# The even layer's mixer in another order: index products inside the projection of queries and keys, index sums on VectorE alone, conv ahead of values, three attention heads inside the value projection, and a masked minimum as softmax bias

## What is computed

```python
proj = h @ w_in      # q, k, v (512 each), q_idx 1024, k_idx 64, w_idx 16, gate_b, gate_c, x_in (512 each)
q, k, q_idx, k_idx = partial_rope(...)
rel   = relu(einsum('bqhd,bsd->bqhs', q_idx, k_idx))        # 16 index heads, 64 wide
score = where(causal, einsum('bqhs,bqh->bqs', rel, w_idx), -inf)
sel   = top_k(score, 64)                                    # keys that each query may see
attn  = softmax(where(selected & causal, q @ k.T * 64**-0.5, -inf)) @ v     # 8 heads
conv  = gate_b * causal_conv_width_3(gate_c * x_in)
mix   = concatenate([attn, conv]) @ w_out
x     = x + rms_norm(mix) * gain
```

## Time and profile before

| | |
|---|---|
| median of 3 runs | 1078.1 us (1076.7 to 1078.5) |
| the profiled execution | 1079.2 us, its span 1077.4 us |
| TensorE busy, matmuls | 1041.1 us, 97% |
| VectorE busy | 660.3 us, 61% |
| ScalarE busy | 562.0 us, 52% |
| GpSimd busy | 103.3 us, 10% |
| DMA | 176.3 MB, 164 GB/s on average |
| granted TensorE clock, mean of the span | 0.989 |

### The profile page before, as it was taken

The page is one execution under the profiler, slowest core; times in us unless marked ns, Lnnn a source line. Parts: engine busy times, 40 slices in busy tenths (PEclk is TensorE's granted clock), DMA queues, the critical chain, the costliest instruction groups (busy, mean ns, idle before and its releaser), DMA issues.

```text
span 1077.4 us, 13860 instructions
## 1 busy us (share of the span) xinstructions
PE 1041.1 (97%) x5074; PEld 872.3 (81%) x5074; DVE 660.3 (61%) x1034; ACT 562.0 (52%) x853; POOL 103.3 (10%) x128
## 2 busy tenths in 40 slices
PE   7999999999999999999989999999998999999997
PEld 6888878887888888788867888888898878888886
DVE  5575665456645555758686855555469767555453
ACT  6466455436554544644544755444366557444541
POOL 2010101001000000202740100000051001000000
PEclk9999999999999999999979999999999999999999
DMA  8746126414545455544422465454246035555521
GB/s 335 283 161 232 53 99 228 148 40 176 183 182 219 157 195 195 194 154 155 157 78 78 183 228 185 171 200 173 91 145 233 29 118 215 179 200 186 195 79 39
DMA packets 28462, 176.29 MB, mean 164 GB/s; under 512 B 3249, under 2 KB 3393, under 8 KB 9985
## 3 DMA queue, kind: packets, MB, share of 16 engines
q1 hardware_dynamic: 26784, 170.08, 43.4%
q0 software_dynamic: 1456, 5.48, 1.4%
q10 hardware_dynamic: 176, 0.13, 0.0%
HBM read 174.62 MB, written 1.05 MB: 163 GB/s over the span
## 4 chain that ended last, share of the span: by engine, by line
PE 83%; DVE 9%; issue 3%; ACT 3%; POOL 2%; DMA 1%; SPq 0%; DVEq 0%; ACTq 0%; POOLq 0%
PE PS L1560 71%; PE PS L1664 3%; PE PS L1629 3%; PE PS L1681 2%; DVE w_lo L1041 2%; PE PS L1771 2%; ACT w_hi L598 2%; DVE w_lo L1035 1%; PE PS L1672 1%; DMA x<-in_x 1%; DVE arena L1074 1%; POOL h L505 1%; DVE h L1406 1%; POOL arena L498 1%; ACT work L678 0%
## 5 line engine op out<-in xcount | busy, mean ns | idle before, releaser
L1041 DVE SCALAR_TENSOR_TENSOR w_lo<-w_raw,gcol,w_hi 128x512 fp32r<-128x512 f32 (+4 forms) x318 | 264.8, 890 | 206.5 <-ACT w_hi L598 205.9
L598 ACT ACTIVATE w_hi<-w_raw,gcol 128x512 fp32r<-128x512 f32 (+4 forms) x326 | 244.5, 817 | 103.1 <-PE PS L1560 102.2
L1560 PE MATMUL PS<-w_hi,hT_hi 128*128 128x512 f32 (+2 forms) x888 | 243.4, 394 | 6.9 <-DVE hT_lo L1056 2.6
L1560 PE MATMUL PS<-w_hi,hT_lo 128*128 128x512 f32 (+2 forms) x888 | 236.3, 386 | 0.0
L1560 PE MATMUL PS<-w_lo,hT_hi 128*128 128x512 f32 (+2 forms) x888 | 234.9, 385 | 0.3 <-DVE w_lo L1041 0.2
L1560 PEld LDWEIGHTS PS<-w_hi,hT_hi 128*128 128x128 f32 x888 | 162.1, 190 | 38.5 <-DVE hT_lo L1056 3.5
L1560 PEld LDWEIGHTS PS<-w_lo,hT_hi 128*128 128x128 f32 x888 | 165.0, 189 | 33.8 <-DVE w_lo L1041 0.9
L1560 PEld LDWEIGHTS PS<-w_hi,hT_lo 128*128 128x128 f32 x888 | 165.8, 190 | 32.8
L1035 DVE TENSOR_TENSOR w_lo<-w_raw,w_hi 128x2048 fp32r<-128x2048 f32 (+1 forms) x70 | 135.7, 1954 | 83.6 <-ACT w_hi L598 83.6
L598 ACT ACTIVATE w_hi<-w_raw 128x2048 fp32r<-128x2048 f32 (+1 forms) x70 | 114.6, 1643 | 106.7 <-PE PS L1560 106.7
L1560 PE MATMUL PS<-w_hi,gT_hi 128*128 128x512 f32 x408 | 113.9, 392 | 0.0
(11 more groups left out here) (169 smaller groups left out, 821.9 us busy)
## 6 DMA issues: line engine op xcount, KB each, us to landing
w_raw<-in_w SPq DMA_DIRECT2D x64, 1024.0 KB, 4.8
w_raw<-in_w_gu SPq DMA_DIRECT2D x22, 1024.0 KB, 4.8
w_raw<-in_w_in SPq DMA_DIRECT2D x11, 1024.0 KB, 7.4
w_raw<-in_w_dn SPq DMA_DIRECT2D x22, 512.0 KB, 5.1
w_raw<-in_w_mem_k SPq DMA_DIRECT2D x4, 1024.0 KB, 4.8
w_raw<-in_w_out SPq DMA_DIRECT2D x4, 1024.0 KB, 4.8
w_raw<-in_w_cq SPq DMA_DIRECT2D x4, 1024.0 KB, 4.8
w_raw<-in_w_mem_v SPq DMA_DIRECT2D x4, 1024.0 KB, 4.9
```

The source lines that it names most:

```text
L598: ins = act.activation(high, source, ACT.Copy, scale=1.0 if col is None else gcol[:, col + TURNED * k:col + TURNED * k + 1])
L1041: ins = dve.scalar_tensor_tensor(out=lo, in0=raw, scalar=gcol[:, col + TURNED * k:col + TURNED * k + 1], in1=hi, op0=ALU.mult, op1=ALU.sub ...
L1560: mm = pe.matmul(bank(t, j)[:, 0:width], rows[:, kc0 + k, tok], w[:, s, at:at + width], start=begin and i == 0, stop=end and i == 2)
```

## The change

It does the same matmuls, transposes and reads, in another order and with some of the elementwise work on another engine:

- **Index.** `turn_index` moves to (0, 1) of the projection of queries and keys, and the 12 banks of index products stand in it three at a time. ScalarE copies all turned banks there. Its relus write to 12 places (`INDEX_HOME`), and wait for no sum. VectorE makes the sums of both tiles; GpSimd's `index_sum` is gone. Tile 0's search stands between the sums of banks 5 and 6, tile 1's behind the rotation of queries and keys.
- **Conv ahead of values.** `w_cx` is loaded and projected ahead of `w_vg`, both unit by unit (`by_unit`: both tiles of a unit one after the other). The turn of queries and keys stands in the conv projection, that of gate_c * x_in in the value projection.
- **Heads inside.** Scores of heads 0, 1 and 2 and the turn of head 0 stand inside the value projection.
- **Gate.** It is turned behind head 3 into the free PSUM banks 0 and 1, and ScalarE copies it. The conv's multiply waits for it (`gate_copied`), and the subtraction to `hT_lo` is GpSimd's.
- **Bias.** In masked attentions the reducing instruction scales by -scale and takes the minimum, which is the bias itself; the `tensor_scalar` is gone, and each tile is signalled by itself (`maxed` counts tiles).
- **Output projection.** Order (0,0), (0,1), (1,0), (0,2), (0,3), (1,1), (1,2), (1,3); the attention rows are turned ahead of (1, 0), the stream's first tile ahead of (1, 3).
- With two turn banks fewer, `mla` swaps its score and turn banks.

```diff
@@ GpSimd
-            def index_sum():
...
             def convolve():
...
-                for i in range(4):
+                for i in range(2):
                     tb_done(pool, CONV_BANK + i)
...
+                pool.wait_ge(gate_copied, TT)
                 pool.tensor_tensor(y_conv, y_conv, gbT, ALU.mult).then_inc(conv_ready, 1)
+                for c in range(4):
+                    pool.wait_ge(conv_high, c + 1)
+                    pool.tensor_tensor(hT_lo[:, 4 + c, :], y_conv[:, c, :], hT_hi[:, 4 + c, :].bitcast(F32), ALU.subtract).then_inc(conv_low, 1)
@@ ScalarE
+            attention(dsa, [0])
+            evict(0, rows2(vg_tok), even_rows)
+            attention(dsa, [1, 2], False)
+            evict(1, rows2(vg_tok), even_rows)
+            attention(dsa, [3, 4], False)
+            for t in range(TT):
+                act.wait_ge(gate_turned, t + 1)
+                act.activation(gbT[:, :, token_cols(t)], PS[:, t, :].rearrange("p (b m) -> p b m", m=P), ACT.Copy).then_inc(gate_copied, 1)
+            attention(dsa, [5, 6], False)
...
+            high_conv(0, 2)
+            attention(dsa, [7], False)
+            high_conv(2, 4)
@@ VectorE, attention
-                            steps.mark(dve.tensor_tensor_reduce(
-                                out=a.S[hd % 3][:, c0:c1], in0=PS[:, a.score_bank + hd % 2, c0:c1], in1=a.mask[t], scale=1.0,
-                                scalar=PICKED, op0=ALU.add, op1=ALU.max, accum_out=a.mx[:, hd, t:t + 1]))
+                            dve.tensor_tensor_reduce(
+                                out=a.S[hd % 3][:, c0:c1], in0=PS[:, a.score_bank + hd % 2, c0:c1], in1=a.mask[t], scale=-a.scale,
+                                scalar=-PICKED, op0=ALU.add, op1=ALU.min, accum_out=a.nb[:, hd, t:t + 1]).then_inc(a.maxed, 1)
@@ VectorE, even mixer
-            after_group(4)
+            after_group(4, ahead=2)
             rotate(heads_of(qi_tok, 64), 0, 8, cos3, sin3).then_inc(h_ready, 1)
-            after_group(1)
+            after_group(1, ahead=1)
...
+            index_sum(0, 6)
             steps.link(dve.tensor_tensor(score[:, 0:P], score[:, 0:P], causal[:, P:2 * P], ALU.add))
             largest(0)
+            index_sum(6, 8)
+            split_to(n["used"])
+            index_sum(8, 10)
+            split_to(n["used"] + 2)
+            index_sum(10, 12)
...
             rotate(heads_of(qk_tok, 64), 0, 8, cos3, sin3).then_inc(h_ready, 1)
...
             largest(1)
@@ TensorE
-            project(4, 2, wide, copies=2, hooks={(1, 1): after_h(turn_index, 2)})
-            turned(4)
-            turned(5)
-            index_products(0, 4)
-            project(4, 2, wide, copies=2, hooks={(0, 1): lambda: index_products(4, 6), (0, 2): lambda: index_products(6, 8),
-                                                 (1, 1): lambda: index_products(8, 10), (1, 2): lambda: index_products(10, 12)})
-            project(4, 2, wide, copies=2, hooks={(1, 1): after_h(lambda: turn_rows(qk_tok, False))})
-            turn_parts((vg_tok, 512))
-            turn_half(cx_tok, 0)
-            turned(4)
-            attention(dsa)
+            project(4, 2, wide, copies=2, hooks={(0, 1): after_h(turn_index, 2), (0, 2): first_index, (0, 3): lambda: index_products(3, 6),
+                                                 (1, 0): lambda: index_products(6, 9), (1, 1): lambda: index_products(9, 12)})
+            project(4, 2, wide, copies=2, order=by_unit, hooks={(0, 2): after_h(lambda: turn_rows(qk_tok, False))})
+            project(4, 2, wide, copies=2, order=by_unit, hooks={(0, 1): lambda: turn_half(cx_tok, 0), (1, 2): first_heads,
+                                                                (0, 3): lambda: attention(dsa, [1]), (1, 3): lambda: attention(dsa, [2])})
+            copied()
+            attention(dsa, [3])
+            for t in range(TT):
+                for b in range(4):
+                    mm = pe.transpose(PS[:, t, P * b:P * (b + 1)], vg_tok[:, t, 512 + P * b:512 + P * (b + 1)], ident[:])
+                mm.then_inc(gate_turned, 1)
+            attention(dsa, range(4, dsa.H + 3))
             pe.wait_ge(conv_low, 4)
-            project(4, 2, wide, kc0=4, chunks=KC, hooks={(0, 2): attention_rows, (1, 2): tile0})
+            project(4, 2, wide, kc0=4, chunks=KC, hooks={(1, 0): lambda: turn_half(h, 0), (0, 2): lambda: turned(2), (1, 3): tile0},
+                    order=[(0, 0), (0, 1), (1, 0), (0, 2), (0, 3), (1, 1), (1, 2), (1, 3)])
```

181 lines of the change are left out of this document (95 added, 86 removed).

## The result

| | before | after |
|---|---|---|
| median | 1078.3 us (4 runs, 1076.7 to 1079.9) | 1060.9 us (4 runs, 1060.6 to 1062.2) |
| profiled execution, its span | 1079.2, 1077.4 us | 1060.7, 1058.9 us |
| TensorE busy, matmuls | 1041.1 us, 97% | 1032.3 us, 97% |
| VectorE, ScalarE, GpSimd busy | 660.3, 562.0, 103.3 us | 647.0, 565.5, 85.4 us |
| granted TensorE clock | 0.989 | 0.996 |

The ratio is 0.9841, 95% interval 0.9824 to 0.9858. Forecast were 1065.0 us and 1061.5 to 1071.5: the direction was right, and the gain, 17.4 us for 13.3, was larger than the range allowed, by 0.6 us.

The account below looks back on a forecast made before the run. The prediction took TensorE's idle and slow time as the bound. Its terms, -1.6 + 0 - 9.7 - 1.6 - 0.4 = -13.3 us, took the median of 1078.1 to 1064.8, given as 1065.0, range 1061.5 to 1071.5 us.

Parts of the forecast that it names:

- Term 3: Even layer's heads, 547.1 to 574.5 us: 17.7 us in place of 27.4, at the full clock; -9.7 us.
- the one new stop: Even layer's heads: TensorE stops until ScalarE has evicted the second tile, 1.5 us.
- the conv's chain: Even layer: gate copies, GpSimd's multiply, roundings and subtractions end at 562.1 us, TensorE's last round at 562.3.
- A: Even layer: GpSimd's conv comes last and TensorE stops ahead of the output projection; +3.3 us, 1068.3; chance 0.15.
- B: Even layer: VectorE is late at the rotation of queries and keys; +5 us at the bound, 1070; chance 0.08.
- E: A quarter of the gain is lost in small waits at new places between products; 1068 to 1070 us; chance 0.07.
- D: Mixer's start: low clock holds, so transposes and index products take twice as long; until 490 adds 22, 1087 us; chance 0.03.
- Term 5: Other layers: a bias per tile starts the first layer's late exponential 0.4 us sooner, last layer gains nothing; -0.4 us.
- Term 1: Turn of index queries and keys, even layer: TensorE's waits of 1.5 us for a bank and 0.16 go; -1.6 us.
- Term 4: Even layer's output projection: the second tile's unit 0 covers the attention rows' rounding and subtraction, a 1.6 us stop; -1.6 us.
- Term 2: Index sums: VectorE takes 16 from GpSimd at 0.60 us each, hidden by 0.8 us of cover; 0, bound +5.
- Rival C: Even layer's heads: TensorE's clock falls at the new stop and the small matmuls behind; +5.5 us, 1070.5; chance 0.09.

Follow-up runs that it names:

- conv behind the heads: The kernel before, old bias kept, with GpSimd's conv held back until the last exponential of the even layer's heads; 1086.9 us, ratio 1.0081.

## Why the prediction was right and wrong

**Right:** the bound (TensorE's idle and slow time), the stretch of Term 3 as the largest term by far, the one new stop and its engine (1.5 forecast, 1.36 measured), the conv's chain (562.1 forecast against TensorE's 562.3, a margin of 0.2; measured 558.5 against 558.9, 0.4: both came 3.5 us sooner, and the order held by little), and the clock at 1.00 over the heads. Rivals A, B and E did not come; D did not either: the clock falls at the mixer's start as before, and the first unit takes 4.2 us instead of 2.7, as much as before (five units took 15.0 instead of 13.7), but it is back ahead of the transposes.

**The step that failed: Term 5, the bias.** It read that the late exponential "starts about 0.4 us sooner", and of the last layer "nothing to gain". 0.41 us is the share of the `tensor_scalar` in the first layer; the signal for each tile brings another 0.68, since the first tile's exponential no longer waits for the second tile's reduction, and the last rounds gain 0.2. In the last layer a busy share of 25.5 in 26.0 was taken as proof, but the stop ahead of head 3 stood outside that window; before, and after:

```profile
837.21 0.89 PE L1664 MATMUL PS<-arena 128*128 128x128 f32 x4 [1.34 <-issue]
```

```profile
819.03 0.89 PE L1696 MATMUL PS<-arena 128*128 128x128 f32 x4 [0.62 <-issue]
```

Forecast 0.4, measured 1.30 + 0.94 = 2.2. That miss alone takes the time out of the range.

**Term 3 was 1.1 us too small** (9.7, measured 10.8). Its content was 17.7 and is 16.6: heads 3 to 7 with the gate and the last rounds took 12.1 for 12.4, the scores and their turn inside cost 2.3 instead of 2.6 (three times 0.66 of the earlier trace rows and 0.33 for the turn are 2.3; the sum had 2.6), and the stop for the conv rows, 0.3, did not come. Its sum was made by content, and that was sound; its account of what the 27.4 us had consisted of was not. The `tensor_scalar` was left as "inside the stretch", with no price. The runs show that with the stop of 2.4 us still in place the bias was worth 6.0 of them, 5.5 by the `tensor_scalar`'s wait for GpSimd (conv behind the heads): its waits kept TensorE waiting at the low clock, one behind the other. The clock that remains without it costs 1.1. Of the other 3.7 us the stops of 2.4, 0.9 and 0.5, less the new one of 1.4, are 2.4; of the last 1.3 some 0.6 should be the overlap that three stops end (an estimate, at 0.2 each, next paragraph), and the rest I did not take apart.

**Terms 1 and 4 were sized from the waits list:** 1.6 each, measured 2.2 and 1.9 (1.83 when undone). A stop costs what the list shows and the overlap of its two neighbours, 0.15 to 0.24 us each (1.36 for a listed 1.21, 1.83 for 1.62). That is most of Term 4's miss of 0.3 and may be up to 0.5 of Term 1's 0.6, which had two stops to lose. No run puts the index part or the order of the projections back, so Term 1 and the end of the stop of 2.4 us rest on the two traces alone.

**Term 2 was right, for a thicker cover** than worked out: 1.6 us for 0.8. A wide sum took 0.51, not 0.60.

**Rival C had the right mechanism and a threshold that this kernel doesn't reach.** The argument against it, that the first layer ran at 1.00 with a stop of 1.74, holds for single stops of that length and not for longer ones: 2.3 us bring the clock down. Nor for two stops close together: 1.06 and 1.46 us at about 136 us did it in some executions (last section). The stop left in the changed kernel is one of 1.2.

Against the forecast of the medians the 4.1 us are 1.8 by Term 5, 1.1 by Term 3, 0.6 and 0.3 by Terms 1 and 4: 3.8. The rest is within the scatter.
